# First projection: x kept in device memory, eight buffers of weight parts, two slots converted by one operation

## The reference

```python
mod = c_act @ w_ada[l] + b_ada[l]
sh_m, sc_m, gt_m, sh_f, sc_f, gt_f = jnp.split(mod[:, None, :], N_MOD, axis=-1)
h = rmsnorm(x, pre_mix_norm[l]) * (1.0 + sc_m) + sh_m
proj = h @ w_in[l]
o_hg = hgrn2_group(proj[..., :HG_COLS], lb_all[l], hg_norm[l])
o_gdn = gdn_group(proj[..., HG_COLS:], gdn_conv_w[l], gdn_a_log[l], gdn_dt_bias[l], gdn_norm[l])
y = jnp.concatenate([o_hg, o_gdn], axis=-1) @ w_out[l]
x = x + gt_m * rmsnorm(y, post_mix_norm[l])
```

## Time and profile before

| what | before |
|---|---|
| median of 3 runs | 2799.99 us |
| the profiled execution | 2793.93 us |
| its span | 2792.2 us |
| TensorE matmul busy, share of the span | 2668.2 us, 96% |
| TensorE weight load busy | 2383.3 us, 85% |
| VectorE busy | 1963.2 us, 70% |
| ScalarE busy | 1412.5 us, 51% |
| mean DMA rate | 226 GB/s |
| first and last weight copy of the first projection (L1983) | 45.5 and 542.9 us |

### The profile page before, as it was taken

One profiled execution on the slowest core, in us unless ns is written; L12 is line 12 of the kernel. 1 busy time (PEld: TensorE's weight loads), 2 busy tenths in 40 slices (PEclk: granted clock), 3 DMA queues, 4 the chain that ended last, 5 costly groups with the idle time before them and its releaser, 6 DMA issues. The chain is left out here.

```text
span 2792.2 us, 49466 instructions
## 1 busy us (share of the span) xinstructions
PE 2668.2 (96%) x18997; PEld 2383.3 (85%) x18997; DVE 1963.2 (70%) x2822; ACT 1412.5 (51%) x2328; POOL 306.2 (11%) x447
## 2 busy tenths in 40 slices
PE   7899999998999999999998999998999999999998
PEld 4679898887878888999998898887878888889998
DVE  2288996687877777898998576656787655555564
ACT  3355757645455555445444555555344444444454
POOL 1011413121011111121221010001011000000000
PEclk9999999999999999999999999999999999999999
DMA  9777676637488888898993765536578655665564
GB/s 370 296 259 238 222 234 196 210 94 244 148 286 271 280 269 272 314 334 304 328 337 127 191 194 155 150 111 221 188 267 292 223 181 180 193 185 187 176 196 133
DMA packets 290166, 632.39 MB, mean 226 GB/s; under 512 B 30722, under 2 KB 51654, under 8 KB 289734
## 3 DMA queue, kind: packets, MB, share of 16 engines
q1 hardware_dynamic: 239120, 484.78, 52.6%
q0 software_dynamic: 39424, 142.62, 14.7%
q10 hardware_dynamic: 11446, 2.54, 0.6%
HBM read 627.77 MB, written 2.10 MB: 226 GB/s over the span
## 5 line engine op out<-in xcount | busy, mean ns | idle before, releaser
L1149 ACT ACTIVATE weight_parts<-weights 128x1024 fp32r<-128x1024 f32 x584 | 607.3, 1057 | 583.8 <-PE accumulators L1340 248.8
L1229 DVE TENSOR_TENSOR weight_parts<-weights,weight_parts 128x1024 fp32r<-128x1024 f32 x584 | 707.8, 1222 | 271.1 <-ACT weight_parts L1149 269.4
L1329 PE MATMUL accumulators<-h_parts,weight_parts 128*128 128x512 f32 x2816 | 780.2, 399 | 22.3 <-DVE h_parts L1216 8.5
L1329 PEld LDWEIGHTS accumulators<-h_parts,weight_parts 128*128 128x128 f32 x2816 | 487.5, 191 | 92.6 <-DVE h_parts L872 10.1
L1340 PEld LDWEIGHTS accumulators<-h_parts,weight_parts 128*128 128x128 f32 x2944 | 454.4, 191 | 72.2 <-DVE weight_parts L1229 10.7
L1340 PE MATMUL accumulators<-h_parts,weight_parts 128*128 128x256 f32 x2944 | 475.1, 283 | 7.7 <-DVE weight_parts L1229 7.7
L1833 PE MATMUL accumulators<-in_h_parts,in_weight_parts 128*128 128x256 f32 x1024 | 264.4, 290 | 20.5 <-DVE in_weight_parts L2142 20.1
L2142 DVE TENSOR_TENSOR in_weight_parts<-weights,in_weight_parts 128x512 fp32r<-128x512 f32 x256 | 186.6, 748 | 110.4 <-ACT in_weight_parts L1983 109.6
L1835 PE MATMUL accumulators<-in_h_parts,in_weight_parts 128*128 128x256 f32 x1024 | 260.7, 286 | 0.0
L1373 PE MATMUL accumulators<-h_parts,weight_parts 128*128 128x512 f32 x864 | 236.5, 395 | 2.0 <-issue 1.8
L1983 ACT ACTIVATE in_weight_parts<-weights 128x512 fp32r<-128x512 f32 x256 | 154.8, 627 | 146.9 <-PE accumulators L1835 101.7
(11 more groups left out here) (418 smaller groups left out, 3624.7 us busy)
## 6 DMA issues: line engine op xcount, KB each, us to landing
weights<-in_w_ff SPq DMA_DIRECT2D x256, 512.0 KB, 6.0
weights<-in_w_in SPq DMA_DIRECT2D x160, 512.0 KB, 5.3
wide<-in_w_ada SPq DMA_DIRECT2D x112, 512.0 KB, 10.3
h_t<-in_ada_w POOLq DMA_DIRECT2D x112, 512.0 KB, 6.8
weights<-in_ffn_w_gate SPq DMA_DIRECT2D x88, 512.0 KB, 4.5
weights<-in_ffn_w_up SPq DMA_DIRECT2D x88, 512.0 KB, 4.5
weights<-in_ffn_w_down SPq DMA_DIRECT2D x88, 512.0 KB, 4.1
weights<-in_w_out SPq DMA_DIRECT2D x64, 512.0 KB, 5.4
```

The costliest lines, as they stand in the source:

```text
L1149: nc.scalar.activation(w[:, held:held + take, 0, :], core.ring[:, q % RING, k:k + take, :], ACT.Copy).then_inc(core.high_ready, take)
L1229: ins = nc.vector.tensor_tensor(w[:, held:held + take, 1, :], core.ring[:, q % RING, k:k + take, :], w[:, held:held + take, 0, :].bitcast( ...
L1329: nc.tensor.matmul(both(nt), high, x[:, kt].rearrange("p a t -> p (a t)"), start=(kt == 0), stop=False, skip_group_check=True)
```

## The change

After the change ScalarE's queue writes x to a tensor in device memory (`x_kept`) after the conversion of slot 26, and SyncE reads it back at the start of `phase_gdn`. Between the two, the place of x in the on-chip memory holds four more buffers of parts (`in_weight_parts_in_x`). Up to slot 47 everything else is as before. From slot 48 on (`DEEP_SLOT`) the parts alternate between the two sets of four, and ScalarE and VectorE work on two slots in one operation: k = 0 and 1 together, k = 2 and 3 together. Such a copy waits for both halves of a group, and the second subtraction of a group frees both halves at once. The gates' load and the write of x count on one semaphore, and the gates' product and the first use of the new buffers wait for both.

```diff
+X_KEPT_SLOT, DEEP_SLOT = 26, 48
...
+        w_in_x = nc.alloc_sbuf_tensor_at("in_1_weight_parts_in_x", [P, KG, 2, CW], F32R, offset=core.x_at)
...
+        def parts(slot):
+
+            if slot < DEEP_SLOT:
+                return w, slot % KG
+            return (w, slot % (2 * KG)) if slot % (2 * KG) < KG else (w_in_x, slot % (2 * KG) - KG)
+
+        def parts_free(act, slot):
+
+            if DEEP_SLOT + KG <= slot < DEEP_SLOT + 2 * KG:
+                act.wait_ge(core.gates_in_x_moved, 32)
+            elif slot >= KG:
+                act.wait_ge(core.parts_used, slot + 1 - (KG if slot < DEEP_SLOT + KG else 2 * KG))
...
-                pe.wait_ge(s["gates_in"], 16)
+                pe.wait_ge(core.gates_in_x_moved, 32)
...
-                if k < HALVES:
-                    act.wait_ge(core.landed[g % RING][k], 16 * ((st.first + g) // RING + 1))
-                if slot >= KG:
-                    act.wait_ge(core.parts_used, slot - KG + 1)
-                nc.scalar.activation(w[:, k, 0, :], core.ring[:, g % RING, part, :], ACT.Copy
-                                     ).then_inc(core.high_ready, 1)
+                held, at = parts(slot)
+                if slot < DEEP_SLOT:
+                    if k < HALVES:
+                        act.wait_ge(core.landed[g % RING][k], 16 * ((st.first + g) // RING + 1))
+                    parts_free(act, slot)
+                    nc.scalar.activation(held[:, at, 0, :], core.ring[:, g % RING, part, :], ACT.Copy
+                                         ).then_inc(core.high_ready, 1)
+                elif k % 2 == 0:
+                    if k == 0:
+                        for half in range(HALVES):
+                            act.wait_ge(core.landed[g % RING][half], 16 * ((st.first + g) // RING + 1))
+                    parts_free(act, slot + 1)
+                    nc.scalar.activation(held[:, at:at + 2, 0, :], core.ring[:, g % RING, part::2, :], ACT.Copy
+                                         ).then_inc(core.high_ready, 2)
...
-                                      ).then_inc(s["gates_in"], 16)
+                                      ).then_inc(core.gates_in_x_moved, 16)
+                if slot == X_KEPT_SLOT:
+                    act.dma_start(core.x_kept, core.xT[:].rearrange("p a b -> p (a b)")).then_inc(core.gates_in_x_moved, 16)
...
-                dve.wait_ge(core.high_ready, slot + 1)
-                ins = nc.vector.tensor_tensor(w[:, k, 1, :], core.ring[:, g % RING, part, :],
-                                              w[:, k, 0, :].bitcast(F32), ALU.subtract)
-                ins.then_inc(core.used if k >= 2 else core.low_ready, 1)
+                held, at = parts(slot)
+                if slot < DEEP_SLOT:
+                    dve.wait_ge(core.high_ready, slot + 1)
+                    nc.vector.tensor_tensor(held[:, at, 1, :], core.ring[:, g % RING, part, :],
+                                            held[:, at, 0, :].bitcast(F32), ALU.subtract
+                                            ).then_inc(core.used if k >= 2 else core.low_ready, 1)
+                elif k % 2 == 0:
+                    dve.wait_ge(core.high_ready, slot + 2)
+                    nc.vector.tensor_tensor(held[:, at:at + 2, 1, :], core.ring[:, g % RING, part::2, :],
+                                            held[:, at:at + 2, 0, :].bitcast(F32), ALU.subtract
+                                            ).then_inc(core.used if k >= 2 else core.low_ready, 2)
...
+        @block.sync
+        def _(sp):
+            sp.dma_start(core.xT[:].rearrange("p a b -> p (a b)"), core.x_kept).then_inc(core.gates_in_x_moved, 16)
+            sp.wait_ge(core.gates_in_x_moved, 48)
...
+        core.x_at = -(-nc.sbuf_base // 32) * 32
```

11 lines of the change are left out of this document (7 added, 4 removed).

## The result

The changed kernel takes 2813.38 us (median of 7 runs, 2809.4 to 2818.66), the kernel before on the same chip 2799.83 us (7 runs). The ratio is 1.0062, 95% interval 1.0050 to 1.0074. By the ratio it is 17 us slower; the medians of these few runs differ by 13.6 us.

A forecast was written before the change was run, and what follows sets the result against it. It took TensorE's 24.8 us of waits for parts in the first projection as what to win back; -16.0 (eight buffers) + 4.8 (write of x) = -11.2 us from 2799.99 gave 2788.8 us, range 2776 to 2803.

The forecast's parts named there:

- Eight buffers: First projection from slot 49: four more slots of stock remove 16.0 of TensorE's 24.8 us of stalls for parts.
- a discount in two of its stretches: Turn starts keep stock low: only 2.0 of 4.2 us gained from 180 to 256 us, 70% of 4.3 from 371 to 493.
- Both halves at once: Deep stretch, first pair of a group: release to use 7.7 us, VectorE comes after 8.7 us, so no cost.
- Rival C: Loop over the two ring groups becomes the bound at ScalarE's first pair: 22 us lost, 2811 us, chance 11%.
- The write of x: Slots 28 to 33, short of data: the 2.1 MB write delays what TensorE waits for, 4.8 us lost, bounds 0 to 6.6.
- the sign that the write is free: Slot 28 starts at 136 us as before.
- The wait for the write: Gates' product at 149.5 us now waits for x, written by about 148.4 us: no cost.
- The reading back: About 550 us, beside GpSimd's four loads: 5.4 us of DMA, x needed a phase later, no cost.
- Double operations: From slot 48, 104 pairs replace 208 singles per engine: ScalarE saves 21 us, VectorE 16.3, counting only where stock is empty.
- Rival A: VectorE is the bound and buffers add nothing: 5.2 us gained against 4.8 lost, 2799.6 us, chance 17%.

The follow-up runs named there:

- the lighter VectorE: VectorE's w_ada steps in turns 2 to 7 cut from 512 to 64 columns: kernel before 2781.81 us; eight buffers, single operations, write of x 2779.31 us.
- the late emptying: Eight buffers, single operations, write of x; from turn 2 ScalarE empties accumulators behind copies of slots 3 and 4, not 0 and 2: 2794.84 us, 1.0000.
- short loads: Weight loads from in_1's second turn on cut to 128 of 512 columns: kernel before 0.9988; eight buffers, single operations, late emptying 2788.31 us, 0.9976.
- early landings: Same cut of weight loads to a quarter of their columns: whole change 2793.25 us, 0.9991; eight buffers with single operations 2794.65 us, 0.9998.
- the late write in the whole change: Whole change with x written at slot 36 instead of 26, gates' product waiting for the gate columns alone: 2812.76 us, 1.0058.

## Why the prediction was wrong, point by point

- **Eight buffers, 16.0 us gained: this step failed.** The runs give some 4 us, not clear of nothing, and the stalls stayed at 24.7 us. The prediction reasoned from the size of the stock (6.6 us of work against stalls of at most 2.3 us) and took ScalarE's 90.3 us of waiting for TensorE as proof that more buffers would be filled. That wait says only that ScalarE was ahead by four in quiet stretches. It does not say it could be ahead by eight where the stock is needed. Three things stand in the way, the first read from the rows and only in part tested: ScalarE's and VectorE's own order, which ties them slot by slot to TensorE's side products and, at a turn's start, to its last matmul; VectorE's side work, which left no time to get ahead; and the ring of two groups, 79.4 us of waiting for weights in place of 27.9. With the lighter VectorE the buffers were worth 11 us. With the late emptying, buffers and order together were worth 7 us, and with short loads too some 10 us (0.9988 + 0.0025 - 0.9976); how much of that the order alone would give four buffers is not known. The prediction took the turn's start as a discount in two of its stretches; ScalarE's program has that wait in every turn.
- **Both halves at once, nothing: this step failed**, and it turned the sign. The pairs cost 14 us with eight buffers. The prediction counted 7.7 us from release to use against 8.7 us that VectorE left. Both terms were off. The landing was near (6.9 us for both halves, where it had 5.3 + 1.3 = 6.6), but SyncE issues late and ScalarE copies late often enough to bring 7.7 to a mean of 9.1. And the 8.7 let VectorE run at TensorE's pace with nothing but its subtraction at the end, while VectorE's side work stands between the subtractions: it came to the use after 9.9 us, and the round to 14.9 us for eight slots that TensorE does in 13.3.
- **Rival C** was this place and this loop, and its sign, ScalarE's waits for weights and VectorE's behind them, came true. That it was priced 2811 us where 2813 was measured is luck in part: it took the buffers at 16.0 gained, the loop at 22 and the write at 4.8 lost, where the runs show 4, 14 and 7. What it said would decide, a mean landing of both halves above 7.6 us, did not come (6.9); engines that come late filled the margin. It had been given 11% on the belief that the margin of 1 us would hold on average; a margin so thin, in a loop with stretches in which VectorE is 53.3 of 57 us busy, deserved a good deal more.
- **The write of x, 4.8 us lost: near in size, the path in part another.** Measured 7 us on its own (interval 3.6 to 10), 6.5 us by the start of the gate matmuls, at the upper bound of 6.6. The prediction had what TensorE waits for land late. Slot 28's weights did not: with the write alone it started as before, which the prediction had named as the sign that the write is free. The first `w_ada` chunk did (5.9 us later in the change), and TensorE stood behind VectorE for it. The clock fell too, with the write alone to 0.72 from 143 to 155 us where it was 1.00. The Trainium skill (DMA: Bandwidth & Descriptors, Issuing engines are not separate DMA queues) says that transfers of different issuers interleave. Behind the jam they did: from 134 to 146 us ScalarE's queue moved 2.10 MB, SyncE's 1.69 and GpSimd's 1.22. In the jam they did not: from 124 to 131 us SyncE and GpSimd had loads under way, and every packet was ScalarE's. The write itself is no test of that rule, since it stood in ScalarE's own queue behind the gates' load.
- **The wait for the write, nothing: right.** The gate matmuls started at 157.3 us, the write had landed at 145.6.
- **The reading back, nothing: right.** It landed in 8.5 us, and from the projection's end both kernels need the same.
- **Double operations, 21 and 16.3 us saved beside the path: right** in duration (1.05 and 1.22 us), and worthless by themselves: with early landings the change is as fast as single operations, no faster (0.9991 and 0.9998, 2 us apart, within what the runs can tell).
- **Rival A** was nearer the truth about the buffers than the forecast: VectorE's side work sets a good part of the stalls. It was wrong that buffers then add nothing: with the lighter VectorE they added more.

Left open: what the stalls of 15.4 us that stay with a lighter VectorE and four buffers are made of, what the late emptying gives without the eight buffers, and why the late write in the whole change lost half of its gain again.

## What to carry to other kernels

A wait for a free buffer proves that the producer is ahead by the buffers it has; before adding buffers, follow the producer's program to the next thing that it must take from the consumer, since it cannot pass that before the consumer gets there. Merging two small operations of a producer also merges what they wait for and what they release; merge along the unit that is loaded and released, not across it. And a loop (release, issue, landing, copy, side work, release) is to be summed with all of the side work in it, over the slots it serves, against the consumer's pace: a margin of 1 us in 9 is none.
